# A decoder step whose first modulation is loaded and applied in two column halves, with its first two projection tiles interleaved

## The reference

```python
mod = silu(c) @ w_ada + b_ada                # c: 9 vectors (1 prompt, 8 samples); w_ada: 1024 x 6144
shift1, scale1, gate1, shift2, scale2, gate2 = split(mod, 6)
h = rmsnorm(x, g_mix) * (1 + scale1) + shift1        # x: 520 tokens x 1024
z = h @ w_in                                 # 5888 columns: 46 tiles of 128
```

## Time and profile before

| | us |
|---|---|
| median of 3 runs | 789.54 (789.35 to 789.87) |
| profiled execution | 789.53 |
| its span in the trace | 787.8 |
| PE busy | 694.5 (88% of the span) |
| DVE, ACT, POOL busy | 318.0, 165.7, 123.9 |
| first matmul of tile 0 | 41.97 |
| tile 1 begins (L1632) | 50.78 |
| tile 2 begins | 57.34 |

### The profile page before, as it was taken

The page is one execution under the profiler, slowest core; times in us unless marked ns, Lnnn a source line. Parts: engine busy times, 40 slices in busy tenths (PEclk is TensorE's granted clock), DMA queues, the critical chain, the costliest instruction groups (busy, mean ns, idle before and its releaser), DMA issues.

```text
span 787.8 us, 12170 instructions
## 1 busy us (share of the span) xinstructions
PE 694.5 (88%) x5003; PEld 532.7 (68%) x5003; DVE 318.0 (40%) x701; ACT 165.7 (21%) x323; POOL 123.9 (16%) x189
## 2 busy tenths in 40 slices
PE   2589999999999999999999999779999988788820
PEld 1289989879899889999997455555565554455500
DVE  2162232135688773322234765425232322211235
ACT  4062222221154442112110111111111111100001
POOL 2400000410006001000000100123333332222112
PEclk9989999999999999999999999769999999988975
DMA  9843546856143438421105972779999999999873
GB/s 293 331 160 140 215 174 267 324 215 222 54 133 118 151 105 331 169 69 67 55 27 177 415 294 87 255 291 400 415 414 413 411 413 417 416 414 416 356 302 151
DMA packets 40399, 198.48 MB, mean 252 GB/s; under 512 B 8174, under 2 KB 8358, under 8 KB 24720
## 3 DMA queue, kind: packets, MB, share of 16 engines
q1 hardware_dynamic: 31088, 175.42, 57.3%
q0 software_dynamic: 8352, 21.81, 8.0%
q10 hardware_dynamic: 904, 0.47, 0.3%
HBM read 188.54 MB, written 17.40 MB: 261 GB/s over the span
## 4 chain that ended last, share of the span: by engine, by line
PE 81%; DMA 6%; DVE 4%; issue 4%; ACT 2%; SPq 1%; POOL 1%; POOLq 0%; DVEq 0%
PE bank L1632 31%; PE bank L1878 16%; PE bank L1833 7%; PE bank L1900 7%; DMA arena<-in_w_in 5%; PE bank L1776 4%; PE bank L1871 2%; PE bank L1773 2%; PE bank L1570 2%; PE bank L1668 2%; PE bank L1731 1%; PE bank L1794 1%; PE bank L1895 1%; DMA arena<-y_scratch 1%; PE bank L1714 1%
## 5 line engine op out<-in xcount | busy, mean ns | idle before, releaser
L1632 PE MATMUL bank<-h_parts,w_parts 128*128 128x260 f32 x2160 | 273.4, 286 | 0.8 <-DVE w_parts L1068 0.6
L1632 PEld LDWEIGHTS bank<-h_parts,w_parts 128*128 128x128 f32 x2160 | 263.8, 189 | 9.9 <-issue 8.2
L1878 PE MATMUL bank<-arena,arena_b 128*64 128x256 f32 x704 | 89.8, 412 | 13.5 <-issue 9.1
L1068 DVE TENSOR_TENSOR w_parts<-arena,w_parts 128x1024 fp32r<-128x1024 f32 x46 | 56.2, 1222 | 71.3 <-ACT w_parts L897 71.1
L1878 PEld LDWEIGHTS bank<-arena,arena_b 128*64 128x64 f32 x704 | 57.6, 148 | 39.5 <-issue 12.3
L1422 DVE TENSOR_TENSOR arena_b<-bank,arena_b 128x128 f32<-128x128 f32 x32 | 9.3, 292 | 129.8 <-ACT arena_b L1000 129.7
L897 ACT ACTIVATE w_parts<-arena 128x1024 fp32r<-128x1024 f32 x46 | 48.4, 1052 | 55.9 <-DMA arena<-in_w_in 41.9
L829 POOL DMA_INDIRECT y_scratch<-arena_b x32 | 33.2, 1037 | 161.9 <-DVE arena_b L1447 154.4
L1833 PE MATMUL bank<-arena,arena_b 128*128 128x512 f32 x128 | 56.7, 597 | 0.0
L1878 PE MATMUL bank<-arena_b 128*64 128x256 f32 x320 | 40.1, 407 | 6.1 <-issue 5.3
L1900 PE MATMUL bank<-arena,arena_b 128*64 128x512 f32 x176 | 42.3, 593 | 0.8 <-DVE arena_b L1428 0.8
(11 more groups left out here) (301 smaller groups left out, 761.1 us busy)
## 6 DMA issues: line engine op xcount, KB each, us to landing
arena<-in_w_gate_up SPq DMA_DIRECT2D x44, 1024.0 KB, 29.1
arena<-in_w_in SPq DMA_DIRECT2D x46, 512.0 KB, 4.9
arena<-in_w_ada SPq DMA_DIRECT2D x22, 1024.0 KB, 7.2
arena<-in_w_down SPq DMA_DIRECT2D x20, 1024.0 KB
arena_b<-in_w_gate_up SPq DMA_DIRECT2D x20, 1024.0 KB
arena_b<-in_w_down SPq DMA_DIRECT2D x20, 512.0 KB
arena_b<-in_x_prompt SPq DMA_DIRECT2D x8, 512.0 KB, 7.8
arena_b<-q_scratch POOLq DMA_DIRECT2D x3, 1024.0 KB, 5.7
```

The source lines that it names most:

```text
L1068: dve.tensor_tensor(w_parts[:, n % 2, 1], ring[:, n % WRING], w_parts[:, n % 2, 0], ALU.subtract).then_inc(s_wlo, 1)
L1632: ins = pe.matmul(ps[s][:, 0:HALF], w_parts[:, n % 2, wp, k], h_parts[:, hp, k, s * HALF:(s + 1) * HALF], start=(k == 0 and hp == 1), stop ...
L1878: ins = pe.matmul(ps[2 + b][R * hh:R * hh + R, 0:2 * P], hTe[:, b, c * P + jj * R:c * P + jj * R + R], w_gu[slot][jj][:, c, :, hh * P:(hh ...
```

## The change

The first third of `w_ada` is cut by columns into two halves of 4 MB. A half holds `shift1` and `scale1` for 512 features, which is what the four eighths k = 0..3 (or 4..7) of h need. The host lays it out as `w_ada0[half, s]`, four loads of 1 MB each. SP issues the first half, x, the tiles 0 and 1 of `w_in`, then the second half. A half needs `first_step` four times (four matmuls each; the two row blocks of a step stand in separate quarters of bank 6), and `turn_mods` adds the quarters while it transposes. DVE does bias, copy and scaling for each half in `first_out(j)`. PE multiplies tile 0 over k = 0..3, then tile 1 over k = 0..3 with the second half's steps between, and then both tiles over k = 4..7. Tile 1 has banks 3 and 7. The biases come in two sets of four loads. Some semaphores are merged elsewhere; that moves no instruction.

```diff
@@ SP @@
-            for a in range(4):
-                load_ada(a)
-                if a == 0:
-                    for i in range(5):
-                        sp.dma_start(x[0:rows[i], i], xp_v[i] if i < 4 else xs_v).then_inc(s_x[i], 16)
-            load_tile(0)
-            for n in range(1, len(ORDER)):
+            load_first(0)
+            for i in range(5):
+                sp.dma_start(x[0:rows[i], i], xp_v[i] if i < 4 else xs_v).then_inc(s_x[i], 16)
+            for n in range(WRING):
+                load_tile(n)
+            load_first(1)
+            for n in range(WRING, len(ORDER)):
@@ ACT @@
             for k in range(KD):
+                j, cc = k // 4, k % 4
+                if k == 4:
+                    split(1)
+                    for jj in range(4):
+                        act.dma_start(ada_bias[32 * jj:32 * jj + 1 + TS, 4:12].rearrange("p (g s) n -> p g (s n)", g=2),
+                                      b_v[1:3].rearrange("g j n -> j g n")[jj:jj + 1].to_broadcast([1 + TS, 2, 512])
+                                      ).then_inc(s_bada, 16)
+                if cc == 0:
+                    act.wait_ge(s_mod, j + 1)
@@ DVE @@
+            def first_out(j):
+                if j == 0:
+                    dve.wait_ge(s_bada, 64)
+                else:
+                    split(1)
+                dve.wait_ge(s_adamm, 4 * j + 4)
+                dve.tensor_tensor(mods[:, 0:4], cube(ps[6][:], 4), ada_bias[:, 12 * j:12 * j + 4], ALU.add
+                                  ).then_inc(s_adaev, 1)
+                dve.wait_ge(s_modT, j + 1)
...
+                dve.engine_nop().then_inc(s_mod, 1)
+                if j == 0:
+                    split(0)
...
+                for k in range(4 * j, 4 * j + 4):
+                    dve.wait_ge(s_hA, k + 1)
+                    if k % 2:
+                        link(dve.tensor_copy(h_parts[:, 0, k, 0:TP], h_tmp[:, k % 3]))
+                    dve.tensor_tensor(h_parts[:, 1, k, 0:TP], h_tmp[:, k % 3], h_parts[:, 0, k, 0:TP], ALU.subtract
+                                      ).then_inc(s_hD, 1)
@@ PE @@
+            def first_step(half, s):
...
+                for kk in range(2):
+                    for jj in range(2):
+                        q = 32 * (2 * jj + kk)
+                        ins = pe.matmul(ps[6][q:q + 32, :], cvec[:, 2 * s + kk], ada0[half][s][:, kk, jj],
+                                        start=(s == 0), stop=(s == 3), skip_group_check=True)
+            def turn_mods(half):
+                pe.wait_ge(s_adaev, half + 1)
+                for cc in range(4):
+                    ins = pe.matmul((ps[0], ps[6])[half][:, 64 * cc:64 * cc + 64], mods[:, cc], both_quarters,
+                                    start=True, stop=True, skip_group_check=True)
+            for s in range(4):
+                first_step(0, s)
+            pe.wait_ge(s_xn, 5)
...
+            turn_x(0)
+            turn_mods(0)
+            for k in range(1, 4):
+                turn_x(k)
+            for k in range(4):
+                tile_step(0, k)
+                if k < 3:
+                    turn_x(4 + k)
+            first_step(1, 0)
+            first_step(1, 1)
+            for k in range(4):
+                if k == 2:
+                    first_step(1, 2)
+                tile_step(1, k)
+            first_step(1, 3)
+            turn_mods(1)
+            for k in range(4, KD):
+                if k == 5:
+                    turn_x(7)
+                for n in range(2):
+                    tile_step(n, k)
```

More of the change, by code:

```diff
@@ L60 @@
 NEARLY = NCONV + 3
[L61 removed]
+TURNED = (2, 4, 5, 7, 2, 4, 5, 2)
 WRING = 2
@@ L90, in positions, with hybrid_step @@
     return ap[..., q:TP:DIL[1]]
-def hybrid_step(nc, x_prompt, x_sample, kv0, kv1, kv2, cache_conv, c_prompt, c_sample, g_mix, w_ada, b_ada, w_in,
+def hybrid_step(nc, x_prompt, x_sample, kv0, kv1, kv2, cache_conv, c_prompt, c_sample, g_mix, w_ada0, w_ada, b_ada, w_in,
                 conv_w, w_pa, w_pb, w_o, g_ffn, w_router, b_router, w_gate_up, w_down, g_final,
@@ L170, in hybrid_step @@
         wo = [cube(arena[:, wo0_at:wo0_at + 4 * D], KD), cube(region("SPLIT", 0, 4 * D), KD)]
[L171 to L174, removed]
+        ada0 = [[region("SPLIT", (4 + 2 * s) * D, 2 * D) for s in range(4)],
+                [region(("CACHE", "QK")[s // 2], 2 * (s % 2) * D, 2 * D) for s in range(4)]]
+        ada0 = [[r.rearrange("p (k j n) -> p k j n", k=2, j=2) for r in half] for half in ada0]
+        ada = cube(region("CACHE", 0, 4 * D), 2)
         qT = cube(region("QK", 0, AT * T), AT)
@@ L333, in hybrid_step @@
         s_ada = [sem(f"s_ada{i}") for i in range(4)]
-        s_ada_end = sem("s_ada_end")
+        s_adb = [sem(f"s_adb{i}") for i in range(2)]
         s_bada = sem("s_bada")
@@ L1116, in by_rows @@
                 dve.tensor_copy(dst, sm[0:TS, 0:P]).then_inc(s_tok, 1)
-            for n in range(NQKV):
+            for n in range(1, NQKV):
                 split(n + 1)
-                if n:
-                    by_rows(n - 1)
+                by_rows(n - 1)
                 if n in (9, 17):
@@ L1579, in turn_x, with tile_step @@
                 ins.then_inc(s_xT, 1)
-            for a in range(2):
-                ada_step(a)
+            def tile_step(n, k):
+                if k == 0:
+                    pe.wait_ge(s_whi, n + 1)
+                    pe.wait_ge(s_wlo, n + 1)
+                pe.wait_ge(s_hA, k + 1)
+                pe.wait_ge(s_hD, h_done(k))
+                for s in range(2):
+                    for wp, hp in ((0, 1), (0, 0), (1, 0)):
+                        ins = pe.matmul(tile_bank[n][s][:, 0:HALF], w_parts[:, n, wp, k],
+                                        h_parts[:, hp, k, s * HALF:(s + 1) * HALF],
+                                        start=(k == 0 and hp == 1), stop=(k == KD - 1 and wp == 1),
+                                        skip_group_check=True)
+                    if k == KD - 1:
+                        ins.then_inc(s_half, 1)
@@ L1989, in laid_out @@
         out[name] = cached(t[name], s)
-    out |= {name: t[name] for name in ("cache_conv", "c_prompt", "c_sample", "g_mix", "w_ada", "b_ada")}
+    out |= {name: t[name] for name in ("cache_conv", "c_prompt", "c_sample", "g_mix")}
+    first = t["w_ada"][0][:, 0:2 * D].reshape(4, 2, P, 2, 2, 512)
+    out["w_ada0"] = first.transpose(4, 0, 2, 1, 3, 5).reshape(2, 4, P, 2 * D)
+    out["w_ada"] = t["w_ada"][:, :, 2 * D:]
+    out["b_ada"] = t["b_ada"]
     out["w_in"] = w_in[[n for _, n, _ in ORDER]]
```

171 lines of the change are left out of this document (75 added, 96 removed).

## The result

The changed kernel takes 792.03 us (median of 8 runs, 790.77 to 795.02), the kernel before 789.39 us beside it on the same chip (8 runs, 788.17 to 789.94): ratio 1.0040, 95% interval 1.0025 to 1.0056. It is 2.6 us slower. The profiled execution took 793.31 us, its span 791.4.

The account below looks back on a forecast made before the run. PE was taken as bound by weight loads, then a serial bias-turn-scaling piece, then its own tile work. Tile 2's start summed as 55.2 + 1.2 + 1.1 + 0.3 = 57.8, 0.5 later: 790.0 us, own range 788.3 to 791.1, whole 787.1 to 793.4.

Parts of the forecast that it names:

- S: Start of tile 2 on PE, its shift carried one to one to the end: forecast 57.8, 0.5 later than 57.34.
- gap before k = 4: PE's tile work waits uncovered for the second half's bias, turn, scaling and h: 4.4 us.
- X: End of the norm of x: forecast 25.7 (23.6 to 28.5), before the change 21.6.
- X to the first tile step: Small transposes and turn on PE, then DVE's copy, scaling, split, samples and rest of h: 6.0 us.
- clock, first tile steps: First tile step starts at half speed after PE's idle time: 1.2 us, between 0 and 2.6.
- clock, behind the gap: The gap before k = 4 may lower PE's clock again: 1.1 us, between 0 and 3.4.
- The landing of x: Last prompt tile of x, behind 6.0 MB, lands at 20.5 (19.1 to 23.3), with 1.4 us lost to biases.
- The PE work: To tile 2 at full clock: sixteen tile steps at 0.72, four turn_x at 0.44, four second-half steps at 0.87: 16.8 us.
- rival 2: PE's clock falls twice, at the first tile steps and eighths 4 to 6: S +3.2, 792.7 us, chance 0.16.
- Rival 1: PE's clock is back by the first tile step and survives the gap: S -1.8 to -3.5, 787.4 us, chance 0.20.
- Rival 3: The slow stretch of loads does not come from the biases, x lands at 23.3: S +2.8, 792.3 us, chance 0.11.
- Rival 4: DVE waits in full for POOL's six bias instructions, 4.2 us in place of 0.3: +4.4, 793.9 us, chance 0.06.

Follow-up runs that it names:

- e3: Changed kernel with all four second-half steps ahead of tile 1's first eighths, two of these eighths behind turn_mods: 787.28 us, ratio 0.9967 to the kernel before.
- e1: Kernel before, with only the first third's bias rows loaded at the start and the rest behind tile 1: 786.99 us, ratio 0.9967.
- e10: Changed kernel with all biases loaded at the start again: 793.87 us, ratio 1.0055 to the kernel before.
- a2: Changed kernel run once more, unchanged: 791.78 us, ratio 1.0031 to the kernel before.
- e2: Changed kernel with 20 filler matmuls in bank 0 in the gap before k = 4, altering later values: 790.07 us, ratio 1.0012 to the kernel before.
- e5: Changed kernel with tile 0's last eighths ordered to end three tile steps ahead of tile 1's: 791.69 us, ratio 1.0020 to the kernel before.
- e9: Changed kernel with 20 filler matmuls, 180 columns wide, in bank 1 in the gap before k = 4: 790.09 us, ratio 1.0007 to the kernel before.
- e7: Changed kernel with x issued first, second-half steps ahead of tile 1, and tile 0's last eighths ending earlier: 783.68 us, ratio 0.9922 to the kernel before.
- e6: Changed kernel without interleaving, tile 0 over all eight eighths and then tile 1: 789.88 us, ratio 1.0003 to the kernel before.
- e4: Changed kernel with the tiles of x issued ahead of the first half of the weights: 787.15 us, ratio 0.9968 to the kernel before.

## Why the prediction was right or wrong

The forecast was 790.0 with its own range to 791.1; 792.0 lies above that and inside the whole range, to 793.4. The views and the mechanisms held: S carries the shift to the end in the medians (+2.5 at tile 3, +2.6 there; the profiled executions differ by 3.8), x behind the weights is read late, no load is waited for at the second half, there is a bare gap before k = 4, the split of tile 2 stands bare. S was 1.8 too low. By the terms of the sum:

| term | forecast | measured | error |
|---|---|---|---|
| X, end of the norm of x | 25.7 | 25.1 | -0.6 |
| X to the first tile step | 6.0 | 7.1 | +1.1 |
| from there to the end of the second half's last step | 10.6 | 11.7 | +1.1 |
| gap before k = 4 | 4.4 | 4.6 | +0.2 |
| k = 4 to tile 2, at the full clock | 8.5 | 8.4 (e3) | -0.1 |
| clock, first tile steps | 1.2 | 0 | -1.2 |
| clock, behind the gap | 1.1 | 2.7 | +1.6 |
| POOL | 0.3 | 0 | -0.3 |
| S | 57.8 | 59.6 | +1.8 |

The errors add up to 4.0 upward and 2.2 downward. That S missed by 1.8 and no more is in part luck.

**The landing of x** was sized well: 20.9 against 20.5. So was what the biases cost: I let two thirds of them take 2.8 us, and they took 2.6 at the landing of tile 0 of `w_in` (e1) and 2.3 at that of x (e10). **The norm** took 4.2 us from there and not 5.2: the backlog of 0.7 did not build up, and the last multiplication took 0.74, not the 1.01 of before.

**X to the first tile step.** The step that failed is "four of `turn_mods`, three groups of at most the 0.88 of the old turn". The trace counts eight matmuls there, and 1.61 us in the chain at half speed. The transposes of x ran at half speed too, 1.04 for four. I had priced these at the level of the old turn, and put the slow clock on the tile steps behind them, which then ran at full speed. Both errors have one cause: the clock came back during the transposes (at 30.5) and not after.

**The PE work.** Tile steps in pairs between other work take 1.63, so 0.82 each, and the single ones 0.95, 0.82, 0.73 and 0.72 in the chain, where I took the 0.72 of a long row. The four steps of the second half took 3.9 and not 3.5. By these numbers a change from one kind of work to the next costs about a tenth of a microsecond.

**The clock behind the gap** is the largest error and the heart of the miss: "a whole half-speed stretch as long as now, 6.8 us, half lost" was my far end (3.4), and I took 1.1. It is 2.7 in the profiled run and 1.6 in a2. Shown by e2: the gap filled and nothing else changed, 2.7 us come back from k = 4 to tile 2 and 2.5 in S. It is rival 2's second half. Its first half, the clock late for the first tile steps, did not happen in the profiled run but in e3, e5 and e9, where nothing ahead of these steps had been changed, and cost 1.6 to 1.8 us up to the second half's first step.

**Rival 1** had half of its condition, the clock back by the first tile step, and fell with the gap; e2 and e7 show the other half: without a long idle stretch the clock stays up. **Rival 3** fell by e1. **Rival 4**: DVE's two-input operations were not slowed beside POOL; the two casts took 0.62 and 0.51 instead of 0.43, and PE waited for neither, while POOL's table went from 8.37 us to 10.18. By the Trainium skill (SBUF — State Buffer, "Who interferes with whom") a DVE instruction with two inputs in SBUF and a POOL instruction that reads SBUF contend for an exclusive lock. The trace shows POOL slowed and these DVE instructions not (1.22 and 0.69 as before), and POOL's table grew by 1.8 us beside about 4 us of them, less than a full lock would make. (The 0.26 us that the prediction quotes for DVE were a multiplication with one tensor input.)

**Where the gain went.** Ten microseconds sooner at the first tile step, twelve more from there to tile 2: steps of `w_ada` that used to lie in PE's wait for loads (3.9), the gap (4.6), the wait for the split (1.7 more than the 0.5 that the transposes of tile 0 took there before), the clock (2.7, against 1.3 that it cost the kernel before from its first tile step on, an estimate from its steps of 1.65 and 1.24 beside 0.96), a fourth transposition of x (0.4), and the changes of work with the rest (0.3). Undoing single pieces gives 2.5 (x first), 3.9 (steps early) and 2.9 (tile 1 apart) in S, which overlap. Left open: whether the late return of the clock in e3, e5 and e9 has a cause or is chance. In the traces that load x behind the first half, the granted clock fell to 0.50 between 20.2 and 23.0, while PE waited for x; it came back 10.2 us later in the changed kernel, a2, e2, e6 and e10, where it had fallen by 22.2, and 13.7 us later in e3, e5 and e9, where it had fallen at 22.3 to 23.0. That orders the runs and does not explain them. Open too is what makes the low stretch behind the gap 3.4 or 6.8 us long, and what the trace's last microsecond and e4's two groups come from.

## What to carry to other kernels

A stage cut in two pays its serial tail twice: the second pass of bias, turn and scaling stands bare unless work that is ready is kept for it. Here the steps of the second half moved ahead of tile 1's, so that its tile steps lie behind them, gave 3.9 us at S, more than the whole change had lost. Before loading something sooner, look at who reads it next and what else that reader waits for; here the half was read 6.8 us after it was ready, and x paid for it. Where a gap of several microseconds opens on PE, price the slow work behind it as well as the gap.

## What the runs showed of the hardware

- Small broadcast loads on another queue slow the main stream far beyond their bytes. 0.15 MB less of them let tile 0 of `w_in` land 2.6 us sooner (e1), 0.15 MB more let x land 2.3 us later (e10), where 0.15 MB at the undisturbed 422 GB/s are 0.4 us. The Trainium skill (DMA: Bandwidth & Descriptors, "Queues, rings and completion order") lets an engine take its queues in turn by packets; these runs show more than the bytes' own time, and which step of the path costs it was not tried.
- One gap, two prices: in and behind the same 4.6 us gap, whose longest wait of PE is 2.75 us, the granted clock was 0.50 for 6.8 us in one run of the changed kernel and for 3.4 us in another. It cost 2.7 and 1.6 us. With waits of at most 2.2 us (e7) it stayed at 1.00.
- A turn by matmul of plain f32 leaves two matmul records for each call: eight for four calls on 64 columns, 1.81 us at half speed and 1.00 at full speed (e7). Four transposes of 128x128 leave four and take 1.11 and 0.66.
